# Grouped heads with a place for each of six context units, and neighbourhood heads whose weights GpSimd divides before they are turned

## What is computed

```python
# grouped heads: 6 query heads, 2 key heads, all 1280 keys
p = jax.nn.softmax(s, axis=-1)
o = einsum(p, v)                                    # gqa_attend
yb = o * silu(gb)
# neighbourhood heads: 6 heads, keys of an 8 x 16 window with a bias, and 256 context keys
s_nb = where(in_win, einsum(q, k_blk) * scale + bias, -inf)
p = softmax(concatenate([s_nb, s_cx], axis=-1))
yn = (einsum(p_nb, v_blk) + einsum(p_cx, v_ctx)) * silu(gn)
# layer 0 only: the 256 context tokens as queries, over context keys alone
yb_c = gqa_attend(qb_c, kb_c, vb_c) * silu(gb_c)
yn_c = gqa_attend(qn_c, kn_c, vn_c) * silu(gn_c)
```

## Time and profile before

| what | value |
|---|---|
| median of 3 runs | 3744.22 us (3742.95 to 3746.77) |
| the profiled execution's own time | 3747.89 us |
| its span, first to last instruction | 3746.1 us |
| mean granted TensorE clock | 0.988 |
| grouped heads, layer 0 and 1 | 576 to 781 us and 1632 to 1815 us |
| neighbourhood heads, layer 0 and 1 | 931 to 1048 us and 1953 to 2057 us |

### The profile page before, as it was taken

One profiled execution on the slowest core, in us unless ns is written; L12 is line 12 of the kernel. 1 busy time (PEld: TensorE's weight loads), 2 busy tenths in 40 slices (PEclk: granted clock), 3 DMA queues, 4 the chain that ended last, 5 costly groups with the idle time before them and its releaser, 6 DMA issues. The chain is left out here.

```text
span 3746.1 us, 52839 instructions
## 1 busy us (share of the span) xinstructions
PE 3611.0 (96%) x20138; PEld 2422.5 (65%) x20138; DVE 2197.5 (59%) x4341; ACT 1281.6 (34%) x2410; POOL 939.5 (25%) x927
## 2 busy tenths in 40 slices
PE   7999998999999999999999999999999999999998
PEld 4656556789754655477887477556565687458743
DVE  4377444764675377457646661774478645754565
ACT  3355434632622355346326221673322211001100
POOL 2400144665032400256650340003144100000000
PEclk9999999999999999999999999999999999999999
DMA  5101241002022100110020311000001323542344
GB/s 194 48 19 42 98 143 53 1 18 75 2 71 79 48 29 33 57 35 2 18 75 11 114 46 45 23 1 23 23 23 57 113 90 112 202 157 90 110 176 153
DMA packets 108984, 253.79 MB, mean 68 GB/s; under 512 B 5216, under 2 KB 33888, under 8 KB 108352
## 3 DMA queue, kind: packets, MB, share of 16 engines
q1 hardware_dynamic: 102624, 230.28, 17.5%
q10 hardware_dynamic: 4816, 14.16, 1.0%
q0 software_dynamic: 1296, 5.97, 0.4%
HBM read 223.14 MB, written 27.26 MB: 67 GB/s over the span
## 5 line engine op out<-in xcount | busy, mean ns | idle before, releaser
L1003 PE MATMUL ps<-ring,hT 128*128 128x512 f32 (+3 forms) x1296 | 379.4, 449 | 8.0 <-DVE nrm_b L1184 2.9
L1003 PEld LDWEIGHTS ps<-ring,hT 128*128 128x128 f32 x1296 | 220.1, 193 | 146.1 <-issue 124.7
L1535 DVE TENSOR_REDUCE stat_a<-ps 128x1 f32<-128x1280 f32 (+1 forms) x144 | 190.6, 1365 | 153.8 <-PE ps L1381 153.8
L1433 PE MATMUL ps<-hT,ring 128*128 128x512 f32 (+1 forms) x640 | 280.2, 551 | 0.0
L1759 POOL TENSOR_TENSOR P_b<-P_b,stat_b 128x1280 f32<-128x1280 f32 (+1 forms) x108 | 227.8, 2131 | 184.6 <-DVE stat_b L1775 184.6
L2756 PE MATMUL ps<-Wd,const 128*128 128x512 f32 x384 | 185.7, 592 | 0.0
L1475 ACT ACTIVATE YT<-ps,stat_a 128x1280 f32<-128x1280 f32 (+1 forms) x144 | 176.6, 1232 | 25.4 <-DVE stat_a L1535 25.4
L2646 PE MATMUL ps<-Y 128*128 128x256 f32 x768 | 171.1, 379 | 0.9 <-DVE Y L2631 0.5
L2646 PEld LDWEIGHTS ps<-Y 128*128 128x128 f32 x768 | 145.8, 190 | 21.3 <-issue 1.5
L1519 POOL COPY rb_a<-stat_a 128x64 f32<-128x64 f32 x72 | 14.7, 237 | 540.3 <-DVE YT L1548 540.3
L1681 PE MATMUL ps<-const,P_b 128*128 128x128 f32 x984 | 131.3, 280 | 14.3 <-POOL P_b L1759 11.8
(11 more groups left out here) (580 smaller groups left out, 7955.4 us busy)
## 6 DMA issues: line engine op xcount, KB each, us to landing
ring<-in_w_down SPq DMA_DIRECT2D x32, 2048.0 KB, 7.8
ring<-in_w_up SPq DMA_DIRECT2D x16, 2048.0 KB, 8.6
ring<-in_w_in SPq DMA_DIRECT2D x14, 2048.0 KB, 8.0
adaw_b<-in_w_ada SPq DMA_DIRECT2D x16, 1024.0 KB, 5.2
ring<-in_w_out SPq DMA_DIRECT2D x6, 2048.0 KB, 8.5
ring<-in_w_in SPq DMA_DIRECT2D x6, 1536.0 KB, 6.8
gates<-const SPq DMA_DIRECT2D x32, 256.0 KB, 2.3
x<-res SPq DMA_DIRECT2D x16, 512.0 KB, 3.5
```

The lines of the kernel that those rows point to most:

```text
L1003: mm = pe.matmul(ps[:, bank(n), 0:hi - lo], hT[:, k, t * P:(t + 1) * P], w[:, k, lo:hi], start=(k == 0), stop=(k == KC - 1))
L1433: mm = pe.matmul(ps[:, GB, 0:hi - lo], pr.view(i0 + c)[:, k, b % 4 * P:(b % 4 + 1) * P], hT[:, k, lo:hi], start=(k == 0), stop=(k == KC - 1))
L1535: dve.tensor_reduce(st[:, i % 4, m:m + 1], scored_at(i, m), AX, ALU.max, negate=True)\
```

## The change

In the grouped heads each of the six context units gets its own part of `Pb` and `PT`. All twelve exponents of the units come before any copy on ACT; all six maxima come before the reciprocals on DVE; the copies of units 0 to 3 go to DVE; S(6) stands on PE ahead of the transposes of unit 4; all units are turned in bank 7. In the neighbourhood heads POOL divides the weights, `Pb` gets a third place in the seventh block of hT, `spread_recips`, `recips` and the gate's extra product go, the result of a pair lies in the first bank of another pair's scores (`out_at`) and the group of two in the last (`turned_at`), and the order on PE becomes scores of p+2, product of p-2, transposes of p. Copies on ACT come behind the exponents of two pairs later. The statistics have eight places in both stages. The rest of the diff is renamed indices.

```diff
--- before.py
+++ after.py
@@ -1559,36 +1559,6 @@
...
@@ -1608,18 +1578,30 @@
...
         if not full[p]:
-            return [(0, XB if p == small - 1 else YB, 0, "act")]
+            return [(0, YB, 0, "dve" if p < small - 2 else "act")]
         return [(0, XB, 0, "act"), (0, YB, 4, "act"), (1, XB, 8, "dve"), (1, YB, 12, "dve"), (1, ZB, 16, "act")]
...
-    def ahead(p, by):
-
-        if p >= small:
-            return range(p + 1, min(p + 2, n))
-        return [p + by] if p + by < small else [small] if p == small - 2 else []
+    def weights(p, e):
+        if full[p]:
+            return Pb[:, p % 2, e, :]
+        at = (0 if p == 0 else p - 1) * 2 * CTX + e * CTX
+        return Pb[:, min(p, 1)].rearrange("p e n -> p (e n)")[:, at:at + CTX]
+
+    def turned(p, lo, hi):
+        if full[p]:
+            return PT[:, p % 2, lo:hi, :]
+        at = 0 if p == 0 else 4 * (p - 1)
+        return PT[:, min(p, 1), at + lo:at + hi, :]
+
+    def last_in_place_of(p):
+
+        if not full[p]:
+            return None
+        return {small: 0, small + 1: small - 1}.get(p, p - 2) if small else p - 2 if p >= 2 else None
...
             for p in range(small):
-                transposes(p, 0)
                 if p == small - 2:
                     scores(small)
+                transposes(p, 0)
                 if p:
                     weighted(p - 1)
...
         def keep_group(eng, j):
             p, half, bank, lo, by = groups[j]
             eng.wait_ge(*S["pT_ready"](j + 1))
-            if p >= 2:
-                eng.wait_ge(*S["o_ready"](2 * p - 2))
-            dst, src = PT[:, p % 2, lo:lo + 4, :], ps[:, bank, :].rearrange("p (b n) -> p b n", b=4)
+            if last_in_place_of(p) is not None:
+                eng.wait_ge(*S["o_ready"](2 * last_in_place_of(p) + 2))
...
             def exps(p, e):
                 act.wait_ge(*S["neg_max"](2 * p + e + 1))
-                if p >= 2:
-                    act.wait_ge(*S["pT_ready"](g0[p - 1]))
-                act.activation(Pb[:, p % 2, e, 0:nk[p] * P], scored_at(p, e), ACT.Exp, bias=st[:, p % 4, e:e + 1],
-                               accum_out=st[:, p % 4, 2 + e:3 + e]).then_inc(*S["exps"].inc())
+                if last_in_place_of(p) is not None:
+                    act.wait_ge(*S["pT_ready"](g0[last_in_place_of(p) + 1]))
...
-            for p in range(2 if small else 1):
+            for p in range(small):
                 for e in range(2):
                     exps(p, e)
-            for p in range(n):
+            for p in range(small):
                 copies(p, 0)
-                for q in ahead(p, 2):
-                    for e in range(2):
-                        exps(q, e)
+            for e in range(2):
+                exps(small, e)
+            for p in range(small, n):
+                copies(p, 0)
+                for e in range(2):
+                    if p + 1 < n:
+                        exps(p + 1, e)
                 copies(p, 1)
...
-            for p in range(3 if small else 1):
-                maximum(p)
-            for p in range(n):
-                if p <= small:
-                    for e in range(2):
-                        reciprocal(p, e)
-                for q in ahead(p, 3):
-                    maximum(q)
-                if small <= p < n - 1:
-                    reciprocal(p + 1, 0)
-                if p:
-                    outputs(p - 1)
-                if small <= p < n - 1:
-                    reciprocal(p + 1, 1)
+            def keep_groups(p):
                 for j in range(g0[p], g0[p + 1]):
                     if groups[j][4] == "dve":
                         keep_group(dve, j)
+
+            for p in range(small):
+                maximum(p)
+            for p in range(small):
+                if p >= 2:
+                    keep_groups(p - 2)
+                dve.wait_ge(*S["exps"](2 * p + 2))
+                dve.reciprocal(st[:, p % 8, 4:6], st[:, p % 8, 2:4]).then_inc(*S["recips"].inc(2))
+                if p >= 3:
+                    outputs(p - 3)
+            maximum(small)
+            for p in range(small - 3, small) if small else ():
+                outputs(p)
+            for e in range(2):
+                reciprocal(small, e)
+            for p in range(small, n):
+                if p + 1 < n:
+                    maximum(p + 1)
+                    reciprocal(p + 1, 0)
+                if p > small:
+                    outputs(p - 1)
+                if p + 1 < n:
+                    reciprocal(p + 1, 1)
+                keep_groups(p)
             outputs(n - 1)
...
@@ -1817,15 +1813,24 @@
...
+
+    def out_at(p):
+
+        return flat[:, base(p + 3):base(p + 3) + P]
+
+    def turned_at(p, g):
+
+        lo, hi = sizes(p)[g]
+        at = base(p + 1) + 2 * BANK if g == 2 else (XB, YB)[g] * BANK
+        return flat[:, at:at + (hi - lo) * P]
...
+                def last_bank_free():
+                    if p >= 3 and thirds(p - 3):
+                        pe.wait_ge(*S["kept_2"](thirds(p - 3)))
+
                 if p >= 2:
                     pe.wait_ge(*S["exps"](2 * p - 2))
+                if p >= 5:
+                    pe.wait_ge(*S["o_used"](p - 4))
...
+                last_bank_free()
                 score(1, window_at(p, 1), u["near"]).then_inc(*S["scored_1"].inc())
...
-            def transposes(p, late):
-                pe.wait_ge(*S["exps"](2 * p + 2))
-                for g, (lo, hi) in enumerate(sizes(p)):
-                    if (g == 2) != late:
+            def transposes(p):
+                for g in (2, 0, 1):
+                    if g >= len(sizes(p)):
                         continue
+                    lo, hi = sizes(p)[g]
+                    pe.wait_ge(*S["rb_ready"](2 * p + (1 if hi <= nk[p] else 2)))
                     if g == 0 and p:
                         pe.wait_ge(*S["kept_0"](p))
-                        if p >= 2:
-                            pe.wait_ge(*S["r_used"](p - 1))
-                        if thirds(p - 1):
-                            pe.wait_ge(*S["kept_2"](thirds(p - 1)))
-                    elif g == 1:
-                        if p and seconds(p - 1):
-                            pe.wait_ge(*S["kept_1"](seconds(p - 1)))
-                        if p >= 2:
-                            pe.wait_ge(*S["o_used"](p - 1))
+                    elif g == 1 and p and seconds(p - 1):
+                        pe.wait_ge(*S["kept_1"](seconds(p - 1)))
                     elif g == 2:
-                        pe.wait_ge(*S["kept_0"](p + 1))
+                        if p + 1 < n:
+                            pe.wait_ge(*S["exps"](2 * p + 4))
+                        if p >= 2 and thirds(p - 2):
+                            pe.wait_ge(*S["kept_2"](thirds(p - 2)))
...
             def weighted(p):
                 u = pairs[p]
                 pe.wait_ge(*S["kept_0"](p + 1))
-                if seconds(min(p + 1, n - 1)):
-                    pe.wait_ge(*S["kept_1"](seconds(min(p + 1, n - 1))))
+                if seconds(p):
+                    pe.wait_ge(*S["kept_1"](seconds(p)))
                 if thirds(p):
                     pe.wait_ge(*S["kept_2"](thirds(p)))
-                if p:
-                    pe.wait_ge(*S["o_used"](p))
+                if p + 3 < n:
+                    pe.wait_ge(*S["exps"](2 * p + 7))
+                if p >= 2:
+                    pe.wait_ge(*S["o_used"](p - 1))
...
             for p in range(n):
-                transposes(p, False)
                 if p + 2 < n:
                     scores(p + 2)
-                transposes(p, True)
-                if p:
-                    recips(p - 1, p)
-                    weighted(p - 1)
-            recips(n - 1, n)
+                if p >= 2:
+                    weighted(p - 2)
+                transposes(p)
+            weighted(n - 2)
             weighted(n - 1)
...
 
         @block.scalar
         def _(act):
             def exps(p, e):
                 act.wait_ge(*S["neg_max"](p + 1))
-                if p >= 2:
-                    act.wait_ge(*S["turned_0"](p - 1))
-                    if seconds(p - 2):
-                        act.wait_ge(*S["turned_1"](seconds(p - 2)))
-                    if thirds(p - 2):
-                        act.wait_ge(*S["turned_2"](thirds(p - 2)))
...
+                if p >= 3:
+                    act.wait_ge(*S["turned_0"](p - 2))
+                    if seconds(p - 3):
+                        act.wait_ge(*S["turned_1"](seconds(p - 3)))
+                    if thirds(p - 3):
+                        act.wait_ge(*S["turned_2"](thirds(p - 3)))
...
-            for p in range(n):
+            def copies(p):
                 act.wait_ge(*S["turned_0"](p + 1))
                 act.activation(*keep_group(act, p, 0), ACT.Copy).then_inc(*S["kept_0"].inc())
                 if len(sizes(p)) >= 2:
                     act.wait_ge(*S["turned_1"](seconds(p)))
```

(85 more changed lines are left out.)

57 lines of the change are left out of this document (17 added, 40 removed).

## The result

| | before | after |
|---|---|---|
| median | 3743.59 us (3742.51 to 3746.77, 4 runs) | 3718.52 us (3715.90 to 3720.65, 4 runs) |
| profiled execution, its span | 3747.89, 3746.1 us | 3719.09, 3717.3 us |

The ratio is 0.9929, with a 95% interval from 0.9917 to 0.9942: about 25 us faster.

A forecast was written before the change was run, and what follows sets the result against it. TensorE's own list was taken to bound neighbourhood pairs, chained waits the context units. Gains of 9 (context units) and 7.6 us (11.2 from steady pairs less 3.6 at the ends) took 3744.2 to 3727.6 us, range 3719 to 3739.

The forecast's parts named there:

- So a boundary costs 0.13: Interior neighbourhood pairs: one more boundary between transpose groups on TensorE adds 0.13 us a pair.
- Bound by PE's own list, and only what leaves it pays: Neighbourhood heads: TensorE's instruction list sets the 4.24 us of an interior pair; only removals from it save time.
- Nothing there waits for an engine: Interior neighbourhood pair: TensorE is busy all of 4.24 us, and the gaps between its instructions are issue.
- The price of R: Neighbourhood heads: removing TensorE's turn of the reciprocals saves 0.31 us an interior pair, 0.26 an edge or context pair.
- Part 3: Ends of the neighbourhood stages: with one more pair in flight, filling and draining lose 3.6 us net.
- GpSimd hidden: Neighbourhood heads: GpSimd's two divisions, 2.5 us a pair, are hidden by TensorE's 4 us.
- a line for width 640: Neighbourhood heads: a line between widths 256 (0.612 us) and 1280 (2.320) gives 1.25 us for GpSimd's 640-wide division.
- Part 1: Layer 0 grouped heads, six context units: own places and new order gain 9 us, bounds 5 and 11.
- A: Neighbourhood pairs: the ring of maxima and exponents, 3.35 us around, becomes the bound at 4.24; total 3738.8 us; chance 0.14.
- B: Neighbourhood pairs: VectorE's bias additions wait 0.8 us each for GpSimd's SBUF reads; total 3769 us; chance 0.06.
- C: Context units: still chained, first full scores start near 591 (sign: after 590), 4.5 us gained; total 3732 us; chance 0.12.
- no boundary cost: Steady neighbourhood pairs: upper bound of 15.8 us gained, in place of 11.2, if transpose group boundaries cost nothing.

The follow-up runs named there:

- boundaries: Kernel after, each group of four transposes cut in two by a signal and two met waits: neighbourhood stages 106.52 and 94.11 us, no change.
- two_apart: Kernel after, with the transposes' group of two between scores and products, as before the change: neighbourhood stages 109.70 and 97.21 us, 6.29 us more.
- one_more: Kernel after, with one more transpose ahead of every neighbourhood pair's first group of four: stages 108.91 and 96.57 us, 4.86 us more; execution 3720.64 us.
- dve_divides: Kernel after, with VectorE in place of GpSimd dividing the neighbourhood heads' weights: stages 119.64 and 102.81 us, 21.8 us more; execution 3734.84 us.

## Why the prediction was wrong where it was
- **"So a boundary costs 0.13"**, the step that failed. It was read off one row, T8's loads spanning 0.97 where two groups of four should take 0.84, and it was added to the list of every interior pair. A boundary costs nothing (`boundaries`), and eight transposes in a row take 0.86 (`two_apart`). The other 0.11 was PE's wait for DVE's output of the product, which shared its bank with the second group of four; the trace of the kernel before shows it. The new order asks for nothing that is so fresh, so the 0.11 went as well. A pair takes 3.86 us, not 4.06: 36 x 0.20 = 7.2 us of the 12.25 by which the neighbourhood heads were missed.
- **Bound by PE's own list, and only what leaves it pays.** Right but for that wait: PE is busy 3.85 of 3.85 us after. "Nothing there waits for an engine" was too strong: neither the merged row nor PE's busy time shows a pause of 0.1 us.
- **The price of R, 0.31 an interior pair.** It was near, its explanation wasn't. R itself is 0.09 (`one_more`), and 0.17 is one change of shape less (`two_apart`), in every pair. With the wait of 0.11 an interior pair gains 0.38, and the prediction's own sum with 0.38 and 0.26 gives 13.7 + 4.7 = 18.4 in place of 11.2. Other rows of eight than those of the steady interior pairs had longer waits, 1.9 us more in all: 20.3.
- **Part 3, the ends, 3.6 us lost.** Wrong in size. From the first scores to S(6) layer 0 took 15.3 us, not 16.3 as forecast (16.9 before), and layer 1 18.7, not 19.5 (21.3 before). From the last scores to the next stage it is 11.46 us in both layers (11.72 and 12.01 before), 12.2 was forecast. These are 3.3 us of the miss. The list's 20.3 less the 0.3 that is left for the ends comes to 20.0; 19.85 was measured.
- **GpSimd hidden; a line for width 640.** Right: 1.25 predicted, 1.255 measured, 1.04 and 1.041 for 512. The full pairs of the grouped heads, priced at nothing, kept their length: layer 1 took 181.15 us before and after.
- **Part 1, 9 us.** 7.2 to 10.4 by profiles (205.1 to 206.9 before, 196.5 to 197.9 after). S(6) was forecast 12.1 us behind the stage's start and came at 14.3. The half clock was assumed for S(6) and fell on units 1 to 3 instead, so these took 2.1 us each, not 1.4; S(6) itself ran in 2.42, not 4.64, and gave that back. S(7), forecast at 2.42, took 3.48 as before (the granted clock was 0.50 again from 596 to 599), so S(8) came 7.9 us behind it, not 7.0, and 1.2 later than forecast. That the total came near 9 is in part luck: two errors of over 2 us cancel.
- **Rivals.** A didn't occur, but its ring is real: with two divisions of 0.55 in it the period goes to 4.16 (`dve_divides`). B didn't occur: 561 ns before and after for the bias addition. The rule of the Trainium skill (SBUF — State Buffer, Who interferes with whom), by which a VectorE instruction with one SBUF input, outside its two-port modes, doesn't contend with GpSimd, agrees with it. C did occur by its own sign, S(6) 14.3 us behind the start where 590 meant 14.1, and its reason was right (slow units, though by the clock and not by the chain). Its price wasn't: 4.5 us gained, against 7.5.

The range was too narrow at its lower end, where the bound "no boundary cost" (15.8) was known and should have stood with a smaller loss at the ends.

## What to carry to other kernels
Where PE's list is the bound, count changes of tile shape in it, not only instructions: one change less was worth twice the instruction removed (0.175 and 0.09 us). The slower engine was free here because PE asks for its result only behind the scores of two more pairs; give the buffer and the order for that first, and look at what each reciprocal, copy or output stands behind in its queue. Price a term from a row that holds it alone. Where a merged row is longer than its count of instructions should take, look at the single starts: here a wait was taken for a fixed cost.

## What was not expected of the hardware
- A change of tile shape on PE costs 0.17 us (0.175 by 36 pairs), and 0.33 behind the scores (64 by 128); a signal and two met waits between transposes cost nothing.
- PE's clock was 0.50 for six us of unbroken work at 583 to 589, behind 5.6 us (577.40 to 583) in which it worked 1.7. With 2.7 us of filler in that time it stayed at 1.00.
- VectorE multiplies 640 SBUF values a lane by one number in 0.55 us, GpSimd in 1.255.
- The next transposes started 0.115 us after the end of the VectorE instruction that they waited for, in 43 rows.
- Untouched stages come out at one of a few lengths, 92.2, 93.7 to 93.9 or 95.1 us in one of them, from profile to profile.
